# Two transformer blocks in one Trainium2 program: one product of the later query rotation changes its engine, and three weight rows are made over six rounds instead of three

## The reference

```python
def mixer_mla_sb(x, w_in, q_norm_g, w_uq, kv_norm_g, w_ukv, w_out, cos, sin):
    b, s, _ = x.shape
    h = x @ w_in
    c_q, c_kv, k_rope, sb_qkv = jnp.split(h, [Q_LORA, Q_LORA + KV_LORA, IN_A], axis=-1)
    q = (rms_norm(c_q, q_norm_g) @ w_uq).reshape(b, s, MLA_HEADS, MLA_NOPE + MLA_ROPE).transpose(0, 2, 1, 3)
    q_nope, q_rope = jnp.split(q, [MLA_NOPE], axis=-1)
    q = jnp.concatenate([q_nope, apply_rope(q_rope, cos, sin)], -1)
    ...
    o_a = sweep_query_blocks(lambda qb, i: mla_block(qb, i, k_a, v_a), q)
    q_b, k_b, v_b = sb_qkv.reshape(b, s, 3, SB_HEADS, SB_DIM).transpose(2, 0, 3, 1, 4)
    o_b = sweep_query_blocks(lambda qb, i: stick_breaking_block(qb, i, k_b, v_b), q_b)
    return jnp.concatenate([o_a, o_b], -1) @ w_out
```

## Time and profile before

| | us |
|---|---|
| three runs | 1417.07, 1416.36, 1417.62 (median 1417.07) |
| profiled execution, its own time | 1416.97 |
| its span | 1415.2 |
| PE busy | 1389.9 (98%) |
| DVE busy | 1020.8 (72%) |
| ACT busy | 933.0 (66%) |
| POOL busy | 391.2 (28%) |

### The profile page before, as it was taken

One profiled execution on the slowest core, in us unless ns is written; L12 is line 12 of the kernel. 1 busy time (PEld: TensorE's weight loads), 2 busy tenths in 40 slices (PEclk: granted clock), 3 DMA queues, 4 the chain that ended last, 5 costly groups with the idle time before them and its releaser, 6 DMA issues.

```text
span 1415.2 us, 30766 instructions
## 1 busy us (share of the span) xinstructions
PE 1389.9 (98%) x11080; PEld 1345.6 (95%) x11080; DVE 1020.8 (72%) x1653; ACT 933.0 (66%) x1569; POOL 391.2 (28%) x389
## 2 busy tenths in 40 slices
PE   9999999999999999999999999999999999999998
PEld 7899889999999999999999899999999989999998
DVE  7867766888748888887488857665478876766557
ACT  5633437655876576558867766557878787655866
POOL 4343002332303243334053224212034401421203
PEclk9999999999999999999999999999999999999999
DMA  6533215555665655666745236555655615655662
GB/s 217 177 105 102 64 37 162 169 174 177 194 194 162 180 164 164 178 177 185 206 153 187 61 105 190 181 179 171 203 160 166 208 47 152 199 186 182 188 191 93
DMA packets 62728, 226.04 MB, mean 160 GB/s; under 512 B 6960, under 2 KB 8240, under 8 KB 62640
## 3 DMA queue, kind: packets, MB, share of 16 engines
q1 hardware_dynamic: 61776, 221.87, 51.4%
q10 hardware_dynamic: 864, 3.01, 0.6%
HBM read 223.80 MB, written 1.05 MB: 159 GB/s over the span
## 4 chain that ended last, share of the span: by engine, by line
PE 68%; DVE 18%; issue 6%; ACT 5%; DMA 1%; DVEq 1%; POOL 0%; SPq 0%; ACTq 0%
PE bank L425 18%; PE bank L426 18%; PE bank L427 18%; DVE w_lo L1747 7%; DVE cv L2143 2%; PE bank L474 1%; DVE x_lo L1775 1%; ACT w_hi L1128 1%; DVE tu L1798 1%; PE bank L463 1%; PE bank L467 1%; PE bank L885 1%; PE bank L886 1%; PE bank L887 1%; DVE tg L1798 1%
## 5 line engine op out<-in xcount | busy, mean ns | idle before, releaser
L425 PE MATMUL bank<-x_hi,w_hi 128*128 128x258 f32 (+6 forms) x2096 | 600.8, 287 | 4.4 <-DVE w_lo L1747 2.0
L426 PE MATMUL bank<-x_lo,w_hi 128*128 128x258 f32 (+6 forms) x2096 | 592.9, 283 | 0.0
L427 PE MATMUL bank<-x_hi,w_lo 128*128 128x258 f32 (+6 forms) x2096 | 592.9, 283 | 0.0
L1747 DVE TENSOR_TENSOR w_lo<-raw,w_hi 128x1024 fp32r<-128x1024 f32 x295 | 374.7, 1285 | 47.3 <-ACT w_hi L1128 32.8
L425 PEld LDWEIGHTS bank<-x_hi,w_hi 128*128 128x128 f32 x2096 | 395.5, 189 | 13.1 <-issue 9.9
L1128 ACT ACTIVATE w_hi<-raw 128x1024 fp32r<-128x1024 f32 x299 | 313.3, 1053 | 131.0 <-PE bank L427 107.9
L426 PEld LDWEIGHTS bank<-x_lo,w_hi 128*128 128x128 f32 x2096 | 396.0, 189 | 0.4
L427 PEld LDWEIGHTS bank<-x_hi,w_lo 128*128 128x128 f32 x2096 | 395.8, 189 | 0.0
L1745 DVE SCALAR_TENSOR_TENSOR w_lo<-raw,negmean,w_hi 128x1024 fp32r<-128x1024 f32 x120 | 159.9, 1335 | 140.6 <-ACT w_hi L1126 139.4
L427 PE MATMUL bank<-a_hi,w_lo 128*128 (+2 forms) x704 | 198.0, 281 | 0.0
L426 PE MATMUL bank<-a_lo,w_hi 128*128 (+2 forms) x704 | 197.9, 281 | 0.0
(11 more groups left out here) (456 smaller groups left out, 2229.9 us busy)
## 6 DMA issues: line engine op xcount, KB each, us to landing
raw<-w SPq DMA_DIRECT2D x419, 512.0 KB, 3.7
h<-h SPq DMA_DIRECT2D x2, 544.0 KB, 5.7
out<-h SPq DMA_DIRECT2D x8, 128.0 KB, 1.9
T<-cs ACTq DMA_DIRECT2D x1, 960.0 KB, 5.7
con_b<-cb ACTq DMA_DIRECT2D x1, 712.0 KB, 4.5
smx<-pin ACTq DMA_DIRECT2D x1, 512.0 KB, 5.3
con_g<-ca ACTq DMA_DIRECT2D x1, 421.5 KB, 6.4
prm<-par ACTq DMA_DIRECT2D x1, 202.0 KB, 4.5
```

Of the source, the lines that this page charges most:

```text
L425: pe.matmul(o, wh, xh, start=first, stop=False)
L426: pe.matmul(o, wh, xl, start=False, stop=False)
L427: return pe.matmul(o, wl, xh, start=False, stop=last)
L1747: V.tensor_tensor(w_lo[:, slot, :], raw[:, slot, :], w_hi[:, slot, :].bitcast(F32), ALU.subtract).then_inc(S("lo_ready"), 1)
```

## The change

VectorE gets one instruction more, behind its own rotation of heads 0 to 3: the product of heads 4 to 7 with the cosines, once they are copied. GpSimd loses that product. Its first step, the product with the sines, no longer waits for `q_rope`; its sum waits for its own product, for VectorE's, and for `q_rope`. In the rounds, the low halves of rows 0, 1, 2 are made in rounds 1, 3, 5, and the high halves of rows 1, 2, 3 in rounds 2, 4, 6; before, each of rounds 1, 2, 3 had one of both.

```diff
@@ -2322,6 +2322,8 @@
             v.then_inc(S("k_copied"), 1)
             ahead(U["m_ukn"], U["m_ukn"])
             q_ropes(0)
+            dve.wait_ge(S("q_copied"), 2)
+            V.tensor_tensor(q_m[rope_rows, 4:8, :], q_m[rope_rows, 4:8, :], CBv("rope", rope_rows).unsqueeze(1).to_broadcast([32, 4, SEQ]), ALU.mult).then_inc(S("q_turned"), 1)
 
             def smallest(hd, base, scale, mask):
 
@@ -2428,9 +2430,10 @@
                     mla_norm(i)
                 if i + 1 < 8:
                     mla_max(i + 1)
-                if 1 <= i < 4:
-                    ahead(U["m_ukn"] + i, U["m_ukn"] + i)
-                    row_high(i)
+                if i in (1, 3, 5):
+                    ahead(U["m_ukn"] + (i + 1) // 2, U["m_ukn"] + (i + 1) // 2)
+                if i in (2, 4, 6):
+                    row_high(i // 2)
                 if i >= 2 and i % 2 == 0:
                     mixed_low(4 + i // 2 - 1, acc[(i // 2 - 1) % 2])
                 if i >= 3 and i % 2:
@@ -2682,11 +2685,10 @@
             rope_rows, swap_rows = slice(64, 96), slice(96, 128)
             q, t = q_m[:, 4:8, :], q_t[:, 4:8, :]
             pool.wait_ge(S("q_copied"), 2)
+            G.tensor_tensor(t[rope_rows], q[swap_rows], turn(swap_rows), ALU.mult).then_inc(S("q_swapped"), 1)
+            pool.wait_ge(S("q_swapped"), 1)
+            pool.wait_ge(S("q_turned"), 1)
             pool.wait_ge(S("q_rope"), 1)
-            G.tensor_tensor(t[rope_rows], q[swap_rows], turn(swap_rows), ALU.mult).then_inc(S("q_turned"), 1)
-            pool.wait_ge(S("q_turned"), 1)
-            G.tensor_tensor(q[rope_rows], q[rope_rows], turn(rope_rows), ALU.mult).then_inc(S("q_turned"), 1)
-            pool.wait_ge(S("q_turned"), 2)
             G.tensor_tensor(q[rope_rows], q[rope_rows], t[rope_rows], ALU.add).then_inc(S("q_rope"), 1)
             pool.wait_ge(S("o_split"), KT)
             for j in range(KT):
```

## The result

The changed kernel takes **1420.82 us** (median of 9 runs, 1418.33 to 1421.46) against 1417.03 for the kernel before (9 runs, 1416.36 to 1417.62): ratio 1.0024, 95% interval 1.0016 to 1.0033. That is +3.8 us, slower by more than the 0.2% that can be told from no change; +1.1 was forecast. It lies above the range that the prediction gave, 1415.4 to 1419.9. The profiled execution is one of the nine, 1421.13, span 1419.3, 4.1 more than before.

A forecast was written before the change was run, and what follows sets the result against it. TensorE, 98% busy, was taken to bound the kernel, with VectorE setting the pace for three rounds. Terms 2.0 - 0.2 - 0.1 - 0.5 - 0.6 + 0.1 + 0.4 = +1.1 us gave 1418.1 us, range 1415.4 to 1419.9.

The forecast's parts named there:

- moved product: VectorE's product for heads 4 to 7, held at the port by GpSimd's swap: 3.4 us instead of 1.2.
- swap: GpSimd's product with the sines goes first at the port: starts near 783.5, lasts about 3.0 us.
- first sums: TensorE's sums before the first scores wait for VectorE's late first remainder: 788.05 instead of 785.91, +2.1 us.
- third remainder: VectorE's stick-breaking remainder after head 2's logarithm: +2.0 us, less 0.2 of ScalarE wait, so +1.8.
- six rounds: Weight row halves spread over rounds 1 to 6: -0.1, -0.5, -0.6, then +0.1 and +0.4 us.
- sum without the clock: Late chain and rounds added up, with nothing for a clock fall: +1.1 us.
- TensorE's clock: Forecast case has the rounds keep the upper level, 1.00, despite 2.0 us of TensorE idle: no cost.
- rival 3: TensorE's clock falls after idling 786.1 to 788.05: 3.7 us more, +4.8 in all, 1421.8 us; chance 0.04.
- What is queued behind it: First remainder waits behind the moved product on VectorE, 784.84 to 787.45; sums, scores, exponentials and logits move alike, +2.1 us.
- the stall that goes: First weight product L2382 finds the port free, but the delay uses up its 1.9 us stall: nothing won.
- Rivals 1 and 2: Rounds give nothing back: 1418.8 us, chance 0.10. VectorE keeps the port at the moved product: 1416.0 us, chance 0.15.
- VectorE's busy time: Whole-kernel VectorE busy time grows about 1.5 us: 1.2 of work and 2.2 of held port, less 1.9.

The follow-up runs named there:

- experiment 3: Changed kernel plus eight useless TensorE products filling the idle before the first sums; 1417.97 us.
- experiment 5: Kernel before with only the product moved to VectorE, rows still in three rounds, plus eight useless TensorE products in the idle; 1419.12 us.
- experiment 6: Changed kernel with GpSimd's first product made to wait for VectorE's, so VectorE has the port first; 1415.98 us.
- experiment 8: Kernel before plus six clearings of an unused tile on VectorE between first rotation and first remainder, a plain delay; 1422.42 us.
- experiment 1: Kernel before with only the product moved to VectorE, weight rows still in rounds 1 to 3; 1420.95 us.
- experiment 2: Kernel before with only the weight rows spread over six rounds, rotation untouched; 1416.45 us.
- experiment 9: Kernel before with weight rows in five rounds, alone 1416.24 us; together with the moved product placed behind the first remainder, 1415.50 us.

## Why the prediction was right and where it was wrong

| term | forecast | measured | where |
| --- | --- | --- | --- |
| moved product | 3.4 | 3.41 | timeline after |
| swap: start, length | 783.5, 3.0 | 783.65, 2.98 | timeline after |
| first sums | 788.05, +2.1 | 788.35; 788.28 with the idle filled | after, experiment 3 |
| third remainder | +1.8 | +2.2 | experiment 3 |
| six rounds | -0.7 | -1.15 | experiments 3, 5 |
| sum without the clock | +1.1 | +0.9 | experiment 3 |
| TensorE's clock | 0 (rival 3: +3.7) | +2.85 | after less experiment 3 |
| whole | +1.1 | +3.8 | |

**The product that moves: right.** The engine that waits goes before the follower of the one that holds, as the earlier trace rows had it; experiment 6 shows the other order, worth 4.8 us. The forecast weighed a sentence of the Trainium skill, Perfetto Trace Analysis, section on optimizing Scalar/DVE operations, which names two-port VectorE operations alone as holding the shared port. Read by itself it would leave this product unheld. The trace of the change does not agree with that reading: 3.41 us, against 1.21 in experiment 6, where GpSimd doesn't ask.

**What is queued behind it, and the stall that goes: right**, a little small. In experiment 3 the third remainder is at 794.87 against 792.56, less 0.11 by which that execution was late already at L2316 (783.08 against 782.97): 2.2. That nothing was won by L2382's 1.9 us of stall held too (experiment 6 has it nearly gone, and no remainder sooner).

**Six rounds: right in kind, small in size.** Experiment 3 against the earlier trace rows, from the third remainder to the row stage, falls from +2.3 to 821.61 - 820.45 = +1.16: -1.15, as the medians have it. Two misses, +0.4 and -0.45, cancel by luck, and the sum without the clock comes out within 0.2.

**What failed is the term at nothing for TensorE's clock, that is, the chance of rival 3.** The text counted the idle at 2.0 us, named the clock as what could follow, gave its price, and then gave it 0.04, because "the rounds keep the upper level, 1.00, with many short waits in them". That argued from waits of up to 1.25 us to one of 2.0, beyond every row, and called an absence in one profiled execution evidence. Experiments 3, 6 and 8 show that it decides the verdict: fill the idle and 2.85 us go; make it another way and the fall comes again. With it the kernel is at 1420.82, 1.0 from rival 3's 1421.8 and 2.7 from the forecast's 1418.1. The Trainium skill, TensorE: Matmul & The Clock Gate, Part 1, has idle stretches bring the lower clock; the text quoted it and set it aside as unseen. The trace of the change now agrees, at 0.50 behind a standstill of 2.09 us; the trace of experiment 1, with the same standstill, has no fall.

**Its price, 3.7, was too high.** Measured against experiment 3, interval by interval: first sums to second sums take 5.18 (788.35 to 793.53) instead of 3.30 (788.28 to 791.58), so +1.9; the rest of the shift, to 2.9, lies before the third remainder (797.81 against 794.87, less 0.08 by which this execution was later at L2316), and behind it the distance stays (824.58 against 821.61). The prediction doubled a whole round of TensorE's work. But the stretch at 0.50 was over by 796, while the third remainder came at 797.81, and from 789 to 795 TensorE was busy 5.26 us of 6.

**The range had a slip.** Rivals 1 and 2 with 0.6 of scatter reach from 1415.4 to 1419.4, not 1419.9. The measured time is above either.

**VectorE's busy time** rose by 3.8, not 1.5. The part at hand is as forecast, 3.41 for the product less 1.91 for L2382. Another 2.3 us is on L1747, all over the program (377.0 us in 295 instructions against 374.7), and other kernels here show that sum anywhere from 372.9 to 376.5; it is off the path.

**What stays open** is why the product alone had the fall in some executions only, when the standstill is equally long; and with it how many of the nine runs of the change had it. Only the profiled one shows it in the trace. The times speak for nearly all: eight of the nine are at 1420.28 or above, and the ninth, 1418.33, is within the range of experiment 3. The mean clock listed for each run is a weaker witness. It is 0.997 in the eight and 0.998 in the ninth, and never under 0.998 in experiment 3. But in the profiled execution the fall makes up 6.8 us at 0.50 and the end of the program, where TensorE has no work left, another 2.5 us, while the profiled execution of experiment 8, with the same fall, lists 0.998, and that of experiment 2, with none here, 0.997.

Open as well is why the price differs. With the six rounds the fall costs 2.85. With the rows in three rounds the two groups of experiment 1 are only 1.7 apart (medians 1419.47 and 1421.2), and the whole of it is 1.8 above experiment 5. So in the changed kernel as it ran, the six rounds were worth 0.13 (1420.82 against 1420.95), not the 1.15 that they are worth where the clock holds. No execution of experiment 1 with a fall was traced, so nothing shows where the difference lies.

## What to carry to other kernels

Where a change makes TensorE wait, read off how long it will stand still in one piece, not only how late the next product starts: here the fall behind 2.1 us of standstill cost 2.9, which turned +0.9 into +3.8, while the standstill itself cost nothing beyond the late chain. An idle longer than any in the trace of before has no row that speaks for its being harmless. And before an instruction is given to an engine that shares a port, see who will be waiting at the port when its predecessor ends, and put it behind the instruction that others wait for: the same product, one place later, cost nothing, and the kernel was 5.0 us faster than the changed one. Filling the standstill with useless products got back only 2.85.

## What was not expected of the hardware

The clock also falls elsewhere in single executions, even with no standstill near. In the profiled execution of experiment 2 (1419.24, the slowest of its eleven and 2.8 above their median) the windows show it twice:

```profile
30.00:35.00 5.00, 5.00 (x34) 4.12 (x33) 3.83 (x8) 3.05 (x6) 3.96 (x6) 1.00 0.31 105
...
35.80:39.20 3.40, 3.40 (x16) 3.40 (x16) 2.35 (x4) 2.15 (x5) 1.83 (x2) 0.50 0.67 181
...
506.80:510.20 3.40, 3.40 (x19) 3.40 (x18) 2.12 (x2) 0.00 (x0) 3.40 (x5) 0.50 0.61 166
```

At 35.8 TensorE had been full for 5 us and more; the trace shows no cause. Falls at that place are in the profiled executions of experiment 6 and of both kernels of experiment 9 too. Before the one at 506.8 there was a wait of 1.77 us for VectorE, at a place that exists in every version (1.02 in the kernel before, 1.24 in the changed one, 1.52 in experiment 1):

```profile
506.41 0.39 PE L425 MATMUL bank<-yb_hi,w_hi 128*128 128x258 f32 x1 [1.77 <-DVE w_lo L1745]
```

So waits of 1.22 and 1.52 us were followed by no fall in their traces, 1.77 by one, 2.09 by one in one trace and none in another, 2.78 by one. What decides it in a given execution these traces do not show. It differs between executions of one kernel, and so is likely a part of the scatter between its runs. A single profile of before that shows the clock at 1.00 throughout, as the earlier trace rows did, is no proof that the kernel is not near such a fall.
